# Splitting an up tile: rounding on ScalarE, one whole subtraction on VectorE

## The reference, cut to what matters

```python
top_v, pos = lax.top_k(cand, TOPK)
expert_idx = jnp.take_along_axis(cand_idx, pos, axis=-1)
gates = jax.nn.softmax(top_v, axis=-1)
u = jnp.take(expert_down, idx_blk, axis=0)
act = jax.nn.gelu(jnp.einsum('bpd,bphkd->bphk', h_blk, u))
vv = jnp.take(expert_up, idx_blk, axis=0)
return jnp.einsum('bphk,bphkd->bpd', g_blk * act, vv)
```

## Time and profile before

| | us |
|---|---|
| median of 3 runs | 1895.82 |
| lowest, highest | 1890.52, 1896.05 |
| the profiled execution: time | 1896.35 |
| its span, first to last instruction | 1895.0 |
| PE busy in the span | 1728.0 (91%) |
| DVE busy | 1121.1 (59%) |
| ACT busy | 461.1 (24%) |
| POOL busy | 384.9 (20%) |
| mean granted PE clock | 0.956 |

### The profile page before, as it was taken

One profiled execution on the slowest core, in us unless ns is written; L12 is line 12 of the kernel. 1 busy time (PEld: TensorE's weight loads), 2 busy tenths in 40 slices (PEclk: granted clock), 3 DMA queues, 4 the chain that ended last, 5 costly groups with the idle time before them and its releaser, 6 DMA issues.

```text
span 1895.0 us, 25552 instructions
## 1 busy us (share of the span) xinstructions
PE 1728.0 (91%) x10111; PEld 1289.2 (68%) x10111; DVE 1121.1 (59%) x2297; ACT 461.1 (24%) x825; POOL 384.9 (20%) x241
## 2 busy tenths in 40 slices
PE   6998998998899957869988888899999999999998
PEld 2333554543455447537888888788888888888887
DVE  4774223331243263425992399967778777777776
ACT  1003232121122221111355555511111111111111
POOL 0000000000000110000276422233333333333332
PEclk9999999999899779889999899999999999999999
DMA  9974333333733100142233321245544555454453
GB/s 342 334 269 164 121 120 115 108 134 119 239 111 133 45 1 3 57 148 89 94 111 121 100 72 68 80 170 179 183 165 156 186 171 183 170 173 169 164 173 112
DMA packets 120523, 267.75 MB, mean 141 GB/s; under 512 B 10210, under 2 KB 43346, under 8 KB 120276
## 3 DMA queue, kind: packets, MB, share of 16 engines
q1 hardware_dynamic: 86352, 228.82, 35.0%
q10 hardware_dynamic: 34052, 37.29, 5.8%
HBM read 261.86 MB, written 4.22 MB: 140 GB/s over the span
## 4 chain that ended last, share of the span: by engine, by line
PE 78%; DVE 13%; issue 2%; ACT 2%; DMA 2%; POOL 1%; ACTq 0%; SPq 0%; DVEq 0%; POOLq 0%
PE bank L466 24%; PE bank L869 12%; PE bank L871 12%; PE bank L873 12%; PE bank L881 5%; DVE hot L1515 3%; PE bank L853 3%; DVE ada_acc L990 3%; DVE hot L1513 2%; POOL dT_low L1977 1%; PE bank L911 1%; PE bank L731 1%; PE bank L449 1%; DMA ada_b<-in_b_ada_dram 1%; PE bank L740 1%
## 5 line engine op out<-in xcount | busy, mean ns | idle before, releaser
L466 PE MATMUL bank<-slot,hT 128*128 128x512 f32 (+2 forms) x1088 | 477.9, 595 | 6.2 <-DVE hT L977 2.0
L466 PEld LDWEIGHTS bank<-slot,hT 128*128 128x128 f32 x1088 | 206.9, 194 | 247.2 <-issue 242.2
L1981 POOL TENSOR_TENSOR up_low<-slot,up_high 128x512 fp32r<-128x512 f32 x128 | 229.6, 1794 | 428.9 <-DVE up_high L1430 428.9
L869 PE MATMUL bank<-hT_high,dT_high 128*128 128x256 f32 x1024 | 296.4, 289 | 13.0 <-POOL dT_low L1977 13.0
L871 PE MATMUL bank<-hT_low,dT_high 128*128 128x256 f32 x1024 | 290.8, 284 | 0.0
L873 PE MATMUL bank<-hT_high,dT_low 128*128 128x256 f32 x1024 | 289.3, 283 | 0.0
L869 PE MATMUL bank<-up_high,A_high 128*128 128x512 f32 x512 | 206.2, 403 | 3.4 <-DVE A_low L1433 3.4
L869 PEld LDWEIGHTS bank<-hT_high,dT_high 128*128 128x128 f32 x1024 | 195.8, 191 | 17.5 <-issue 14.6
L871 PE MATMUL bank<-up_low,A_high 128*128 128x512 f32 x512 | 202.3, 395 | 0.0
L873 PE MATMUL bank<-up_high,A_low 128*128 128x512 f32 x512 | 201.6, 394 | 0.0
L1892 ACT CAST dT_high<-bank 128x512 fp32r<-128x512 f32 x256 | 143.9, 595 | 230.4 <-PE bank L881 226.1
(11 more groups left out here) (407 smaller groups left out, 2199.7 us busy)
## 6 DMA issues: line engine op xcount, KB each, us to landing
slot<-in_expert_down_dram SPq DMA_DIRECT2D x128, 512.0 KB, 4.5
slot<-in_expert_up_dram SPq DMA_DIRECT2D x128, 512.0 KB, 3.8
slot<-in_w_in_dram SPq DMA_DIRECT2D x27, 2048.0 KB, 8.0
P<-in_w_ada_dram ACTq DMA_DIRECT2D x24, 1024.0 KB
slot<-in_w_out_dram SPq DMA_DIRECT2D x4, 2048.0 KB, 7.8
slot<-in_w_query_dram SPq DMA_DIRECT2D x4, 2048.0 KB, 7.9
slot<-in_w_branch_sb_dram SPq DMA_DIRECT2D x2, 2048.0 KB, 7.8
slot<-in_w_branch_ret_dram SPq DMA_DIRECT2D x2, 2048.0 KB, 8.5
```

Source lines behind the costliest of these rows:

```text
L466: m = pe.matmul(sums, lhsT=lhs[:, k, t * P:(t + 1) * P], rhs=w[:, k, :], start=(k == 0), stop=(k == w.shape[1] - 1))
L869: pe.matmul(o, lhsT=lhs_high.bitcast(F32R), rhs=rhs_high.bitcast(F32R), start=start, stop=False, skip_group_check=True)
L1981: g.tensor_tensor(up_low[p % 4][:, CW:].bitcast(F32R), up_tile[p % 4][:, CW:], up_hi[p % 2][:, CW:], ALU.subtract).then_inc(up_low_pool, 1)
```

## The change

The rounding of an up tile moves from VectorE to ScalarE, with the waits that belong to it (the tile's load, the up product two steps back, and for the first two tiles GpSimd's last down subtraction, whose buffers `up_hi` takes over). VectorE subtracts all 1024 columns in one operation. GpSimd does nothing in the last part, and TensorE no longer waits for it. On ScalarE's queue the split of tile 0 stands behind the wait for the gelu writes and ahead of the steps; within step `p` the split of `p+1` stands between the turn for `p+2` and the gelu for `p+1`. VectorE's order is the same but for the rounding.

```diff
     def pe_tile_up(p):
         pe.wait_ge(weighed, p + 1)
         pe.wait_ge(up_low_dve, p + 1)
-        pe.wait_ge(up_low_pool, p + 1)
@@
     def v_split_up(p):
-        v.wait_ge(up_in[p % 4], 16 * (p // 4 + 1))
-        if p > 1:
-            v.wait_ge(tile_done, p - 1)
-        else:
-            v.wait_ge(down_low, 2 * AHEAD)
-        v_high(up_hi[p % 2], up_tile[p % 4]).then_inc(up_high, 1)
         v.wait_ge(up_high, p + 1)
-        v_low(up_low[p % 4][:, 0:CW], up_tile[p % 4][:, 0:CW], up_hi[p % 2][:, 0:CW]).then_inc(up_low_dve, 1)
+        v_low(up_low[p % 4], up_tile[p % 4], up_hi[p % 2]).then_inc(up_low_dve, 1)
@@
+    def a_split_up(p):
+        a.wait_ge(up_in[p % 4], 16 * (p // 4 + 1))
+        if p > 1:
+            a.wait_ge(tile_done, p - 1)
+        else:
+            a.wait_ge(down_low, 2 * AHEAD)
+        a.copy(up_hi[p % 2].bitcast(F32R), up_tile[p % 4]).then_inc(up_high, 1)
@@
         for j in range(2):
             a.wait_ge(middle_out[j], 8 * MIDDLE)
+        a_split_up(0)
         for p in range(N_KEYS):
             if p + 2 < N_KEYS and ups[p + 2] >= AHEAD:
                 a_tile_turn(ups[p + 2])
+            if p + 1 < N_KEYS:
+                a_split_up(p + 1)
             if p + 1 < N_KEYS and ups[p + 1] >= AHEAD:
                 a_tile_gelu(ups[p + 1])
@@
-        for p in range(N_KEYS):
-            g.wait_ge(up_high, p + 1)
-            g.tensor_tensor(up_low[p % 4][:, CW:].bitcast(F32R), up_tile[p % 4][:, CW:], up_hi[p % 2][:, CW:],
-                            ALU.subtract).then_inc(up_low_pool, 1)
```

More of the change, by code:

```diff
@@ L160, in program @@
     h_high_ready, h_low_ready = sem("h_high_ready"), sem("h_low_ready")
-    down_high, down_low, up_high, up_low_dve, up_low_pool = (
-        sem("down_high"), sem("down_low"), sem("up_high"), sem("up_low_dve"), sem("up_low_pool"))
+    down_high, down_low, up_high, up_low_dve = (
+        sem("down_high"), sem("down_low"), sem("up_high"), sem("up_low_dve"))
     weighed, tile_done = sem("weighed"), sem("tile_done")
```

## The result

| | before | after |
|---|---|---|
| median, us | 1893.76 | 1897.82 |
| lowest to highest | 1887.96 to 1898.47 | 1896.25 to 1901.66 |
| runs | 20 | 20 |
| profiled execution: time, span | 1896.35, 1895.0 | 1896.4, 1895.1 |

The changed kernel takes 1.0024 of the time of the kernel before, with a 95% interval of 1.0016 to 1.0031: slower by 0.24%, some 4.5 us, and within the 0.3% that I took as the edge. The forecast was 5.1 us and +0.27%.

A forecast was written before the change was run, and what follows sets the result against it. TensorE, busy 100 of 100 us, was taken as the bound. At the handover 3.5 us of delay plus 1.6 us of slow clock made 5.1, so 1896.35 became 1901.5 us (1900.9 against the median); range 1895 to 1905.

The forecast's parts named there:

- PE bounds the last part and no split is on its path: Last part: TensorE busy 100 of 100 us and waiting for no split, so cheaper splits gain nothing there.
- Sizes of the operations: Per up tile: ScalarE cast 1.06 us, VectorE's whole subtraction 1.23; VectorE's load falls to 57%, ScalarE's rises to 39%.
- ScalarE's cover of 1.0 + 0.9 us: Steady state: a split may come 1.0 us later before gelu, plus 0.9 before the up product ends, without delaying TensorE.
- ScalarE's wait for the up product two back is met: Steady state: that product precedes, on TensorE, transposes ScalarE has just handled, so this new wait costs nothing.
- The handover is the cost: From coefficients to first up tile: split 0 waits for all gelu writes, delaying up tile 1 and the end by 5.1 us.
- Its size: Handover: up tile 1 starts 3.5 us late, plus 1.6 us of slow clock, together 5.1; bounds 3.5 to 6.8.
- rival C: Handover: the last gelu write lands in 2.0 us, not 5.03, so delay is 1.6 to 3.3 us, about 1898; chance 0.09.
- The slow clock is on the path now: Up tile 0 after 8.8 us idle: half-clock matmuls, formerly hidden under the wait for tile 1, cost 1.6 us.
- The bound in which the clock stays low through all twelve matmuls: Handover's upper bound: all twelve matmuls of up tile 0 and the transposes run slow, 6.8 us in total.
- A: Last part: lighter SBUF traffic shortens TensorE's 0.231 us matmul step, up to 26 us less, giving 1875; chance 0.06.
- B: Steady state: ScalarE becomes late and its splits hold up gelu in 80 late tiles, 1909 and up; chance 0.10.

The follow-up runs named there:

- the old handover and the new steady state: Changed kernel, but up tiles 0 and 1 split by VectorE and GpSimd as before, without the wait for gelu writes; 0.9996 of the kernel before.
- the kernel with two casts: Changed kernel with ScalarE's rounding cast of each up tile done twice, one after the other; 1.0036 of the kernel before.
- the trace with staged matmuls: Changed kernel with 24 extra TensorE matmuls ahead of up tile 0, a wait for ScalarE's cast, then 8 more; 1.0021 of the kernel before.
- both kernels with extra matmuls: Changed kernel with extra TensorE matmuls ahead of up tile 0: 30 in one block, 1.0025 of the kernel before; 24 and 8 around a wait, 1.0021.

## Why the prediction was right, point by point

- *PE bounds the last part and no split is on its path.* Right: 647.7 us for that part in both kernels, and 0.9996 with the old handover and the new steady state.
- *Sizes of the operations.* Right: cast 1057 ns (1.06 taken), subtraction 1226 ns (1.23), product 425, cast from C 287. DVE took 60 us in the hundred where I had 57, ScalarE 37 where I had 39.
- *ScalarE's cover of 1.0 + 0.9 us.* That there is cover is right, its size is not: 1.08 us more was free and 2.16 us was not, and the tightest steps had 1.37 us. I had taken a step in which the tile's own gelu comes late; the tightest ones are six steps whose gelu is read back from DRAM, where the split follows the turn and the weights follow the split. This erred without a cost, since the cast took 1.06 us as reckoned.
- *ScalarE's wait for the up product two back is met.* Wrong in 46 steps, 97.5 us together. It cost nothing, as PE was in no wait.
- *The handover is the cost.* Right, shown from both sides: the wait alone makes the old kernel as slow as the new one, and moving split 0 ahead of it removes the cost.
- *Its size.* Landing to up tile 0: 3.39 us in the trace, 3.27 reckoned (1235.83 to 1239.1). From tile 0 to tile 1: 5.59 (1233.67 to 1239.26), reckoned 3.64 + 1.6 = 5.24. At an equal landing the delay is then 8.98 - 3.36 = 5.6 us (3.36 is 1235.83 to 1239.19 before), a little over my 5.1. The runs give 4.5. That the sum came so near the 4.5 us is in part luck. The term I took as fixed was the landing: 5.03 us in the trace of before, 3.99, 5.44, 5.24, 5.60 and, in the kernel with two casts, 2.44 in others. When it is short, the old kernel's tile 1 is held by PE instead and the new kernel's moves up with the landing. With a landing after 2.44 us the new tile 1 would start at 1230.80 + 2.44 + 8.98 = 1242.2 and the old one at 1238.1: 4.1 us. That is my rival C, in part; that some executions are of this kind, and that it makes up the missing 0.6 to 1.1 us, is reckoned, not shown. The interval also reaches 5.9 us.
- *The slow clock is on the path now.* Charged at 1.6 us; the trace with staged matmuls gives 1.9. No difference in time shows it: both kernels with extra matmuls took as long as the changed one within their intervals. The bound in which the clock stays low through all twelve matmuls was not idle: two of the experiments' traces show it.
- *Rivals.* C charged the slow clock to the old kernel only: with it in both, its 1.6 us becomes 3.2 (1241.3 against 1238.1). A falls: matmul starts stayed 0.23 us apart with GpSimd idle throughout. B falls at one cast per tile and holds at three.

## What to carry to other kernels

Moving work to an idle engine moves it into that engine's order: look at what it waits for just ahead of the new place. A wait that cost nothing where it stood, because the work behind it was late anyway, can become the start of a whole stage. Where the bound engine has no idle time in a loop, look for gains and losses at the edges of the loop only; there, a pause of the tensor engine cost its own length and, where it was 2.1 us or longer in these traces, slow matmuls behind it.

## What the runs showed of the hardware

- The last write of 128 KB to DRAM took between 2.44 and 5.60 us to land, from one trace to the next, where the fifteen before it took 1.7 to 1.9 us in the kernel before. It lands close behind two loads of 512 KB that SyncE had issued ahead of it: these had landed by 1235.7, 1229.9 and 1231.6 at the latest (before, changed, two casts), the write at 1235.83, 1230.28 and 1232.07. No run here moves those loads, so that they hold up the write is not shown.
- After idle stretches of 2.1 to 10.5 us the granted clock was at half (0.50 from 1234.0 to 1236.5 in the kernel before, starts of 512 columns 0.43 us apart) for part or all of up tile 0; after 0.78, 0.96, 1.41 and 1.59 us it stayed at full. The fall need not come at once: behind 2.24 us idle, the second to the fifth matmul still started 0.23 to 0.24 us apart. How long it lasted didn't follow the length of the pause: 7.82 us idle made tile 0 take 4.79 us, 4.19 us idle made it take 5.26 in two kernels and 4.34 in a third.
- A 128x256 product of two SBUF operands on VectorE took 1103 ns in the mean with GpSimd at work and 425 ns with it idle; a cast of that size out of C 1378 and 287 ns.
- The kernels before and after, which are equal up to there, reached the end of the last early down product 4.5 us apart (1230.35 and 1225.84), as much as the effect. Spans of single profiled executions could not have shown it; distances inside the trace did.
